# A hybrid decoder layer on one core: the prompt's tokens in two parts, the second part's attention issued between the matmuls of the first part's output projection and MLP

## The reference

```python
xn = rmsnorm(h, W['norm_mix'][i]); z = xn @ W['w_in'][i]
(gb, gc, gh, pv, cq, ck, cv, cqi, cwi, cki, dq, dk, dv) = jnp.split(z, cuts, axis=-1)
y_a = gb * causal_dwconv(conv_buf, gc * gh, W['conv_a'][i])
y_b = multiscale_pool(pool_buf, pv, P, W['pool_maps'][i], W['pool_scale'][i])
score = sum over 8 heads of relu(cqi @ cki.T) * cwi          # indexer
_, sel = lax.top_k(score, n_sel)                              # 256 keys of each query
y_c = softmax(cq @ ck[sel].T) @ cv[sel]                       # "dsa", 4 heads
a = softmax(q1 @ k1.T) - lam * softmax(q2 @ k2.T)             # "diff", 4 heads
y_d = rmsnorm(a @ dv)
h = h + concat([y_a, y_b, y_c, y_d]) @ W['w_out'][i]
xn2 = rmsnorm(h, W['norm_ffn'][i])
h = h + (silu(causal_dwconv(ffn_buf, xn2 @ w_gate)) * (xn2 @ w_up)) @ w_down
h = h + (p @ w_ple) * sigmoid(rmsnorm(h) @ w_ple_gate); y = rmsnorm(h)
```

## Time and profile before

| | |
|---|---|
| median of 3 runs | 2059.22 us (2058.13 to 2061.54) |
| the profiled execution, its span | 2056.5 us |
| PE matmul busy | 1782.8 us, 87%, 9933 instructions |
| DVE, ACT busy | 1014.8 us (49%), 629.8 us (31%) |
| moved by DMA | 102.80 MB, mean 50 GB/s |

### The profile page before, as it was taken

The page is one execution under the profiler, slowest core; times in us unless marked ns, Lnnn a source line. Parts: engine busy times, 40 slices in busy tenths (PEclk is TensorE's granted clock), DMA queues, the critical chain, the costliest instruction groups (busy, mean ns, idle before and its releaser), DMA issues.

```text
span 2056.5 us, 26558 instructions
## 1 busy us (share of the span) xinstructions
PE 1782.8 (87%) x9933; PEld 1599.2 (78%) x9933; DVE 1014.8 (49%) x2033; ACT 629.8 (31%) x1083; POOL 39.9 (2%) x43
## 2 busy tenths in 40 slices
PE   3999996847788976998979999999999999998794
PEld 3999983424455665667969999999899899998794
DVE  5113406787778885333344444534443443454643
ACT  3111125555456733443122211121121121113321
POOL 0000000000000002001000000000000000000000
PEclk9999996855566555887989999999999999999897
DMA  3111112111211112113101111111111111120102
GB/s 143 41 51 41 51 53 61 27 41 57 67 42 41 42 41 62 31 32 142 45 27 42 41 52 42 42 42 45 49 41 42 42 42 51 41 67 31 31 31 84
DMA packets 48043, 102.80 MB, mean 50 GB/s; under 512 B 5378, under 2 KB 21762, under 8 KB 47938
## 3 DMA queue, kind: packets, MB, share of 16 engines
q1 hardware_dynamic: 45506, 92.44, 14.4%
q0 software_dynamic: 2432, 8.92, 1.2%
HBM read 93.69 MB, written 7.66 MB: 49 GB/s over the span
## 4 chain that ended last, share of the span: by engine, by line
PE 68%; DVE 13%; issue 9%; ACT 4%; SPq 2%; DMA 2%; POOL 1%; DVEq 0%; POOLq 0%; ACTq 0%
PE ps L213 41%; PE ps L1364 10%; PE ps L533 3%; PE ps L494 2%; PE ps L519 2%; DVE TN L818 2%; PE ps L447 1%; DVE TN L266 1%; DVE Z L971 1%; PE ps L1499 1%; SPq L1101 1%; PE ps L545 1%; PE ps L1185 1%; DMA pages<-in_d_pages 1%; SPq L1102 1%
## 5 line engine op out<-in xcount | busy, mean ns | idle before, releaser
L213 PE MATMUL ps<-xh,wh 128*128 128x352 f32 x1968 | 640.7, 326 | 34.6 <-DVE xl L271 21.6
L213 PE MATMUL ps<-xh,wl 128*128 128x352 f32 x1968 | 638.0, 324 | 0.0
L213 PE MATMUL ps<-xl,wh 128*128 128x352 f32 x1968 | 637.7, 324 | 0.0
L213 PEld LDWEIGHTS ps<-xh,wh 128*128 128x128 f32 x1968 | 372.7, 189 | 40.5 <-issue 26.2
L213 PEld LDWEIGHTS ps<-xh,wl 128*128 128x128 f32 x1968 | 372.7, 189 | 0.0
L213 PEld LDWEIGHTS ps<-xl,wh 128*128 128x128 f32 x1968 | 372.3, 189 | 0.0
L204 ACT ACTIVATE wh<-wr 128x1024 fp32r<-128x1024 f32 x106 | 112.1, 1059 | 849.6 <-PE ps L213 604.8
L208 DVE TENSOR_TENSOR wl<-wr,wh 128x1024 fp32r<-128x1024 f32 x106 | 129.5, 1223 | 431.2 <-ACT wh L204 431.1
L1364 PE MATMUL ps<-ah,wh 128*128 128x352 f32 x528 | 175.3, 332 | 18.0 <-DVE Z L1443 17.9
L1443 DVE TENSOR_TENSOR Z<-Z,ps 128x352 f32<-128x352 f32 x264 | 134.5, 520 | 98.3 <-PE ps L1364 97.8
L1364 PE MATMUL ps<-al,wh 128*128 128x352 f32 x528 | 169.9, 322 | 0.0
(11 more groups left out here) (247 smaller groups left out, 1884.7 us busy)
## 6 DMA issues: line engine op xcount, KB each, us to landing
wr<-in_weights SPq DMA_DIRECT2D x106, 512.0 KB, 3.6
pages<-in_d_pages SPq DMA_DIRECT2D x64, 256.0 KB, 2.9
pages<-in_c_pages SPq DMA_DIRECT2D x64, 96.0 KB, 1.9
Z<-in_xT SPq DMA_DIRECT2D x8, 528.0 KB, 8.7
Z<-in_xT POOLq DMA_DIRECT2D x8, 528.0 KB, 8.1
out_y<-TN SPq DMA_DIRECT2D x8, 528.0 KB, 2.7
arena<-in_c_pages SPq DMA_DIRECT2D x64, 64.0 KB, 1.8
out_d_k<-Z POOLq DMA_DIRECT2D x2, 528.0 KB, 6.5
```

Of the source, the lines that this page charges most:

```text
L213: last = nc.tensor.matmul(out, w_at(w), x_at(x), start=start and t == 0, stop=stop and t == 2)
```

## The change

The 1056 columns are cut into part A (the query tiles 0 to 2, 384 columns) and part B (tiles 3 to 7 and the samples, 672 columns, two pieces of 336). PE now does: norm and the 22 blocks of the projection of part A (`pe_first_projection`); then 380 "places", four to a step of 95 steps, in each of which `pe_mixers` issues one piece of attention or indexer work and `pe_dense` a number of single dense matmuls given by the table `ISSUED`; then output projection, norm and MLP of part B, and embedding, gate and last norm for all columns as before.

- Dense matmuls of the places: part B's projection in places 0 to 123 (1056 matmuls of 336 columns), part A's output projection in 124 to 151 (192 of 384 columns), part A's gate, up and down products from 160 on (1584 of 384 columns; 5 parts in weight for a place up to 267, 9 after).
- Attention of the places: part A in steps 2 to 25, the indexer's scores for part B in 32 to 37, the samples' scores in 38, part B's differential heads and sdiff in 39 to 66, its DSA heads and sdsa in 67 to 90. Part A's top-k search stands in steps 3 to 21; part B's (six arrays, three counted by DVE, three by ACT) in 39 to 66, in 45 pieces over 56 slots, so up to two bits in a step.
- The blocks of the input projection, the output projection, gate, up and down are loaded and split twice, once for each part: 202 block loads, 106 before. The ring of blocks has three slots instead of two.
- The indexer's product and DSA logits are plain f32 with 64 rows for each head, two heads in two row groups, instead of split operands stacked to 128 rows; the two maps of a differential head are issued alternately.
- SP issues weight blocks and page loads in one program order, by places. Keys and values of a DSA page are two loads now. Constants come over POOL's queue. Part B's scores are saved to DRAM, overwritten by their magnitudes for the search, and loaded back before the masks. The search has one junk buffer for its counts, before two in turn.
- The SiLU of part A is made of a tanh and a multiply.

```diff
+TA = 3
+NA = TA * P
+NB = NT - NA
+NBP = SEQ - NA
+CB = NB // 2
+TC = NT // 3
...
+QUANTA = [("pa", n, 0, 24, n) for n in range(NZ)]
+ORDER = list(range(NZ))
+for b in range(NZ):
+    ORDER.append(b)
+    QUANTA += [("pb", b, c, 24, len(ORDER) - 1) for c in range(2)]
+for m in range(KC):
+    ORDER.append(W_OUT + m)
+    QUANTA.append(("out", m, 0, 24, len(ORDER) - 1))
...
+for g in range(GROUPS):
+    add_chunk(2 * g)
+    if g:
+        add_down(g - 1)
+    add_chunk(2 * g + 1)
...
+ITEMS = [("none", 0, 0)] * 2
+for kind in PROMPT:
+    ITEMS += [(kind, i, h) for i in range(TA) for h in range(4)]
+A_END = len(ITEMS)
+IDX_STEP = A_END + 6
+ITEMS += [("none", 0, 0)] * 13
+B_FIRST = len(ITEMS)
+samples_left = list(range(DB))
+for i in TILES:
+    for h in range(4):
+        ITEMS.append(("diff", i, h))
+        if samples_left and (h == 3 or (h == 1 and i > TILES[0])):
+            ITEMS.append(("sdiff", samples_left.pop(0), 0))
+DSA_B = len(ITEMS)
+pairs_left = list(range(DB // 2))
+for i in TILES:
+    for h in range(4):
+        ITEMS.append(("dsa", i, h))
+        if h == 1 and i > TILES[0]:
+            ITEMS.append(("sdsa", pairs_left.pop(0), 0))
+B_END = len(ITEMS)
+ITEMS += [("none", 0, 0)] * 4
+NN = len(ITEMS)
+NPOS = 4 * NN
+UNITS = [(i, a, min(512, (i + 1) * P - a), p) for i in [TA - 1] + TILES for a in range(0, (i + 1) * P, 512) for p in range(4)]
...
+for u in range(NU):
+    if u < NU_A:
+        place = 4 * (u // 2) + u % 2
+    else:
+        v = u - NU_A
+        place = 4 * (IDX_STEP + v // 6) + (0, 0, 1, 1, 2, 3)[v % 6]
+    UNITS_AT.setdefault(place, []).append(u)
...
+PROJ_END = 31
+FFN_STEP = B_FIRST + 1
+ISSUED = {}
+ISSUED |= spread(N_PB, [(p, 1) for p in range(0, 4 * PROJ_END)])
+ISSUED |= {p: n + N_PB for p, n in spread(N_OUT, [(p, 1) for p in range(4 * PROJ_END, 4 * (SIDX_STEP - 1) + 4)]).items()}
+ISSUED |= {p: n + N_PB + N_OUT for p, n in spread(len(MM) - N_PB - N_OUT, [
+    (p, 5.0 if p < 4 * DSA_B else 9.0) for p in range(4 * FFN_STEP, NPOS)]).items()}
+for p in range(NPOS):
+    if p not in ISSUED:
+        ISSUED[p] = ISSUED[p - 1]
...
+B_STAGES = ([("sign", j) for j in range(NTOP)] + list(range(15)) + [("ties", 0), ("ties", 1)] + list(range(15, BITS))
+            + [("mask", NTOP - 1)] + [("mask", j) for j in range(NTOP - 1)])
+def stage_places(stages, first, last):
+    slots = [(n, p) for n in range(first, last) for p in (1, 2)]
+    assert len(stages) <= len(slots)
+    return {slots[k * len(slots) // len(stages)]: s for k, s in enumerate(stages)}
...
+B_STAGE_AT = stage_places(B_STAGES, SIDX_STEP + 1, DSA_B)
...
+        def pe_quantum(pe, n, j):
+            kind, f, c, count, s = QUANTA[n]
+            out = bank(6 + n % 2)
+            if j == 0:
+                pe.wait_ge(w_lo, s + 1)
...
+                if (kind, f) == ("g", 0):
+                    pe.wait_ge(h_out_a, KC)
+                    norm_ffn_a.until(pe, norm_ffn_a.lo, KC)
...
+            elif kind == "pb":
+                cols = slice(0, CB)
+                w, x = three(t, s % 3, (xh_b[:, k, c * CB:(c + 1) * CB], xl_b[:, k, c * CB:(c + 1) * CB]), k)
+            else:
+                cols = slice(0, NA)
+                w, x = three(t, s % 3, (xh_a[:, k], xl_a[:, k]), k)
+            last = nc.tensor.matmul(out[:, cols], w, x, start=j == 0, stop=j == count - 1)
+            if j == count - 1:
+                last.then_inc(dense_mm, 1)
...
+        def pe_dense(pe, place):
+            for a in issue(place):
+                pe_quantum(pe, *MM[a])
...
+        def pe_idx_unit(pe, u):
+            i, a, w, p = UNITS[u]
...
+            if u >= 2:
+                pe.wait_ge(idx_relu, u - 1)
+            for h in range(2):
+                r = slice(HD * h, HD * h + HD)
+                last = nc.tensor.matmul(bank(2 * (u % 2) + h)[:, 0:w], Z[r, QI + p, i * P:(i + 1) * P], Z[r, KI2, a:a + w], start=True, stop=True)
+            last.then_inc(idx_mm, 1)
...
+        def sp_dsa_pages(sp, j):
+            sp.wait_ge(pv_mm, real(ITEMS.index(("sdiff", DB - 1, 0) if j < 2 else ("sdsa", j - 2, 0))) + 1)
+            for b in range(2):
+                r = slice(HD * b, HD * b + HD)
+                for g in range(NPG):
+                    load_page(sp, dsa_keys(j)[r, g * P:(g + 1) * P], lambda i: d["c_pages"][i, 0:HD, 0:P].rearrange("o p c -> p (o c)"),
+                              (2 * j + b) * NPG + g, c_in[j % 2])
+                    load_page(sp, dsa_values(j, b)[:, g], lambda i: d["c_pages"][i, :, P:P + HD].rearrange("o p c -> p (o c)"),
+                              (2 * j + b) * NPG + g, c_in[j % 2])
...
+        DIFF_PAGES_AT = {4 * B_FIRST + 1: 0} | {4 * (ITEMS.index(("sdiff", b - 1, 0)) + 2) + 2: b for b in range(1, DB)}
+        DSA_PAGES_AT = {4 * (ITEMS.index(("sdiff", DB - 1, 0)) + 2) + 2 + j: j for j in range(2)}
+        DSA_PAGES_AT |= {4 * (ITEMS.index(("sdsa", j - 2, 0)) + 2) + 2: j for j in range(2, DB // 2)}
...
+        def sp_second_part(sp):
+            at = {}
+            for s in range(NZ, NFIRST):
+                at.setdefault(max(DONE[LAST_Q[s - 3]], 0), []).append(s)
+            for place in range(NPOS):
+                if place == 0:
+                    sp.wait_ge(dense_mm, NZ)
+                    sp.dma_start(early[:, :], d["early"]).then_inc(s_early, 16)
+                for s in at.get(place, ()):
+                    sp.wait_ge(dense_mm, LAST_Q[s - 3] + 1)
+                    load_block(sp, ORDER[s], s % 3)
+                if place == 4 * IDX_STEP:
+                    sp_idx_pages(sp)
+                if place in DIFF_PAGES_AT:
+                    sp_diff_pages(sp, DIFF_PAGES_AT[place])
+                if place in DSA_PAGES_AT:
+                    sp_dsa_pages(sp, DSA_PAGES_AT[place])
...
+            pe_first_projection(pe)
+            for place in range(NPOS):
+                pe_mixers(pe, place)
+                pe_dense(pe, place)
+            pe_out(pe)
+            norm_ffn_b.pe_sums(pe)
...
-            pe_idx(pe)
-            pe.wait_ge(sscored, 1)
-            pe.wait_ge(idx_relu, len(IDX))
-            for n in range(NI + 6):
-                if n == TAIL + 1:
-                    pe_sdiff_tail(pe)
-                pe_item(pe, n)
-            pe_stage(pe, W_OUT, y_lo_cp, h_out)
-            norm_ffn.pe(pe)
```

More of the change, by code:

```diff
@@ L81, in build @@
+USE_OF = {use: k for k, use in enumerate(USES)}
+TR_OF = {use: sum(a[0] != "so" for a in USES[:k]) for k, use in enumerate(USES)}
 def build(nc, d):
@@ L152, in c_, with early_ @@
             return cst[0:rows, at:at + n]
+        def early_(name, rows=P):
+            at, n = EARLY[name]
+            return early[0:rows, at:at + n]
         def p_(name):
@@ new lines, in norm_signals @@
+        def norm_signals(name):
+            return [sem(f"{name}_{what}") for what in ("squares", "sums", "stat", "std", "diag", "bcast", "scaled", "hi", "lo", "rec")]
+        first_norms, second_norms = norm_signals("norm0"), norm_signals("norm1")
+        tn = lambda a: [a[:, r] for r in range(3)]
+        two = lambda a, n: ps8[:, a:a + n].rearrange("p a b -> p (a b)")
+        norm_a = Norm(first_norms, 0, lambda k: H[:, k, part_a], "g_mix", tn(TN_a), bank(0), bank(1)[:, 0:NA], (xh_a, xl_a))
@@ new lines, in build, with sidx_out, act_idx_samples @@
+        COLS = [(0, 512), (512, 512), (1024, NS)]
+        def sidx_out(g, j, rows, w):
+            return bank(2 * g + j)[rows, 0:w] if j < 2 else bank(5)[rows, 64 * g:64 * g + w]
+        def act_idx_samples(act):
+            act.wait_ge(evac, NZ + 2 * PROJ.index(("qi", 3)) + 2)
+            for par in range(2):
+                for h in range(IDXH):
+                    half = slice(HD * (h % 2), HD * (h % 2) + HD)
+                    last = nc.scalar.activation(qis[HD * par:HD * par + HD, :, 4 * h:4 * h + 4], samples(Z[half, QI + h // 2])[:, par:DB:2], ACT.Copy)
+            last.then_inc(qis_copied, 1)
@@ L1280, in act_mixers, with product_b @@
-        def act_mixers(act):
+        def product_b(pe, first_bank, slot, ready=None):
+            order = [(k, c) for k in range(KC) for c in range(2)] if ready else [(k, c) for c in range(2) for k in range(KC)]
+            for k, c in order:
+                if ready and c == 0:
+                    ready(k)
+                cols = slice(c * CB, (c + 1) * CB)
+                for t in range(3):
+                    w, x = three(t, slot, (xh_b[:, k, cols], xl_b[:, k, cols]), k)
+                    last = nc.tensor.matmul(bank(first_bank + c)[:, 0:CB], w, x, start=k == 0 and t == 0, stop=k == KC - 1 and t == 2)
+            return last
```

2573 lines of the change are left out of this document (1453 added, 1120 removed).

## The result

The changed kernel takes 2175.19 us (median of 4 runs, 2167.58 to 2181.36); beside it the kernel before took 2060.38. The ratio is 1.056, 95% interval 1.053 to 1.059: slower by 115 us, where I forecast slower by some 40. The profiled execution spans 2179.6 us.

A forecast was written before the change was run, and what follows sets the result against it. Dense matmuls at full clock bound two thirds of the span, a chain of waits the middle. Six stages, 125 + 229 + 150 + 405 + 396 + 793 = 2098, plus 2.7 from span to median, gave 2101 us; 8 in 10 range 1975 to 2205.

The forecast's parts named there:

- SP term: Page-load bursts ahead of weight loads in SP's queue make PE wait: 43 us in stage 3, 106 in stage 5.
- stage 4: Places 156 to 267, part B's differential attention, samples and top-k search: DVE-bound, 405 us.
- the diff pages: Page loads in eights, 9 us, claimed hidden by two blocks of lead (over 20 us): 0.
- stage 3: Places 128 to 155, part B's index scores: PE 82, serial tail 25, SP's burst 43, sum 150 us.
- Rival 1: Bursts of page loads are hidden, half of 149 us gone, stage 4 at DVE's bare 368: 1990 us, chance 0.36.
- Stage 2: Places 0 to 127, part B's projection with part A's attention: PE-bound 205 us, with additions 229.
- rival 3: No overlap as claimed; dense PE work adds to DVE's, +60 in stage 4, +30 in stage 5: 2191 us, chance 0.12.
- my three terms: Additions to DVE's work in stage 4: serial counts 9, waits for ACT's counts 20, scores back from DRAM 8 us.
- my own test: Stage 4's signs: DVE over 85% busy, PE's clock near 0.8; forecast wrong if DVE under 80%.
- rival 2: Clock stays low: 0.72 in stage 3 (+32), 0.60 in stage 4 (+40), 0.86 in stage 5 (+35); 2208 us, chance 0.13.
- Stage 5: Places 268 to 379, dense matmuls and DSA: PE-bound 273 us, late-freed banks 17, SP 106, sum 396.
- Stage 6: Tail for part B, output projection, norm, MLP, then embedding, gate and last norm as before: 793 us.

The follow-up runs named there:

- spread: Changed kernel with index pages issued three at a time and DSA pages two at a time between weight loads, no longer in bursts: 2022.53 us, ratio 0.983.
- skip4: Changed kernel with only the first and last dense matmul of each weight block's group falling in places 156 to 267 done: 2166.97 us, ratio 1.052.
- extra4: On top of `spread`, nearly every second dense matmul in stage 4 issued twice, nothing added on DVE and ACT: 2019.61 us, ratio 0.980.
- no_counts: Changed kernel without the counts of part B's top-k search on DVE and ACT: 2107.37 us, ratio 1.023.
- keys: On top of `spread`, differential samples' keys and values loaded apart, the next sample's keys two steps earlier: 1988.54 us, ratio 0.965.
- count_act: On top of `spread`, one more of the top-k search's counts moved from DVE to ACT: 2025.07 us, ratio 0.982.
- lean: On top of `keys`, dense matmuls of part A's MLP weighted 2.6 and 11.5 between stages 4 and 5, not 5 and 9: 1997.98 us, ratio 0.970.

## Why the prediction was right in direction and short in size

The sum came out 82 us short of the profiled span (2098 against 2179.6), so the loss was put at some 40 us where 115 were measured. The SP term accounts for 18 of the 82; the rest lies in the stages' own terms. The step that failed most is in stage 4: the diff pages were priced at 0.

**The SP term was right in kind and 18 us small.** I put 43 + 106 = 149 us on the bursts; the waits in the trace are 69 + 98 = 167, and `spread` got 153 back. It is more than the whole loss of 115. In stage 3 two errors add up, 43 against 69. A page load was priced at 1.13 us; it took 1.25 for the index pages (79.8/64) and 1.17 for the DSA pages (37.4/32), and the DMA instruction alone 0.47 and 0.41, against 0.33 in the earlier trace rows. And the step "PE wants it at place 138, 2.6 steps or 35 us later" took the wrong engine: ACT, in order, wants the block at place 132, 14 us after the burst's start, and holds the ReLU and the exponentials behind it. That stage 3 still came out at 149 for 150 is luck: PE and the tail, 82 + 25 = 107 in the sum, came to 80. Rival 1 counted on two blocks of lead as cover; the early split uses up most of it. `spread`, at 2022.5, shows how far the kernel falls when the bursts don't stop it; rival 1 had 1990.

**Stage 2 is mis-sized by 31 us.** "PE-bound: 205, 4 more for a clock just under 1": PE was busy 227 us at clock 0.93, so PE's own time is the larger part. The rest is waits: 7.1 us for the reloaded residual rows (10 in the sum), 8.7 for a projection result. What PE's extra 22 us are is not settled. The clock accounts for about 15 (205/0.93 is 220). Groups of narrow matmuls may account for the rest; see the last section.

**Stage 4 is the largest miss, 405 against 460.** The form was right: PE's dense part is nearly free (`skip4` -9, `extra4` +12), rival 3 falls, and `no_counts` gives 76 for 93 us of DVE and 98 of ACT. The terms were not. DVE's own work came to 328, not 368: the masked maxima took 48 us, not 59 (L1554 and L1562), the combinations 24, not 38 (L1583 and L1592). DVE's idle time came to 132, not the 37 of my three terms. The largest was priced at 0 by the step "The diff pages come in eights, 9 us, which two blocks of lead (over 20 us there) hide: 0": I asked only who is behind these loads on SP, not who uses them. PE waits 37.3 us for them and DVE 65.2 for the logits that follow; `keys` took 30 us out of the stage by that alone. Of my three terms the trace has 15.1 us of DVE's waits for ACT's counts (20 in the sum) and 3.0 for the scores' return (8). Another 19.3 are waits for the logits of the prompt's heads, which the sum didn't have; what makes up the rest is open. The kernel before had nearly the same two waits, of PE from 297 to 950 us and of DVE from 427 to 760, and I had not set them against the new order:

```profile
PE ps L494 <- DMA pages<-in_d_pages: 33.7, 7, 8.1
...
DVE Z L979 <- PE ps L494: 48.5, 8, 9.2
```

DVE was busy 71%, not over 85, so by my own test I was wrong there. `count_act` and `no_counts` fit one reading of it: a bit is a chain through DVE and ACT, and the stage is held by links that alternate, which no engine's busy sum gives. No run isolates that chain.

**The clock, rival 2.** It was 0.71 in stage 4, between the forecast's 0.8 and the rival's 0.60. PE's work was sized well: 240/0.71 is 338 us, and PE was busy 335. But the price was not the rival's +40: at 0.57 (`skip4`) the stage was no longer, at 0.76 (`extra4`) no shorter. Both runs change PE's work as well, so no run shows the clock's price alone.

**Stage 5: 429 against 396.** The waits behind bursts, 98 against 106, were right. Without them the stage takes 327 (`spread`), where I had 290: PE was busy 294, not 265, and the clock 0.94, not 0.97. The 17 us for banks freed late do not follow from their terms (16 times 1.2 and 0.55 is 28), and no run isolates them. The stage is PE-bound as forecast: PE was busy 90% of it, and `lean`'s 262 more matmuls made it 51 us longer.

**Stage 6: 752 against 793.** The output projection and MLP had almost no waits. The MLP, 1504.3 to 1996.8, is 492.5 us for the 486 of pure matmuls, so 22 of the 28 "of waits as before" did not come. The 14 before the stage came to 4, which lie ahead of its first matmul and so in stage 5; the output projection took 61 and not 59, the norm 16 and not 26. In the MLP of the kernel before, 17.9 of PE's 26.5 us of waits are for DVE's adds into the residual:

```profile
PE ps L1364 <- DVE Z L1443: 17.9, 32, 1.0
```

The changed kernel's MLP has no such wait. I carried over a wait that goes with three banks of 352 columns; part B has two of 336. That this is why it went is argued, not shown.

## What to carry to other kernels

When loads of unlike length share a queue, look for the first engine that touches the late tile in its own order, and price all that stands behind it there; that is sooner than the engine that computes with it. Spreading a burst in small pieces between the urgent loads was worth 153 us here, though ACT still waits 47 us for loads. Of each load ask both who stands behind it and who uses it. In a stage where engines wait for each other, busy sums bound the time from below only. A work item's PE part can be nearly free (227 more: 12 us) while the work that comes with it on other engines costs more than its own length (48 us of DVE work and 19 of ACT: some 60 us).
